# The third and fourth x tile are loaded behind the second half of the modulation weights, with row statistics of their own, and turned half a unit later

## The reference, cut to what matters

```python
def rms_norm(x, g):
    xf = x.astype(jnp.float32)
    y = xf * lax.rsqrt(jnp.mean(xf * xf, axis=-1, keepdims=True) + EPS)
    return (y * g.astype(jnp.float32)).astype(x.dtype)
...
    mod = c @ w_ada + b_ada                      # w_ada is (1024, 3072)
    shift, scale, gate = jnp.split(mod[:, None, :], 3, axis=-1)
    h = rms_norm(x, norm_g) * (1 + scale) + shift
    proj = h @ w_in
```

## Time and profile before

| | |
|---|---|
| median of 3 runs | 1639.85 us (1638.99 to 1643.24) |
| the profiled execution: its time | 1640.34 us |
| the profiled execution: its span | 1638.5 us |
| PE busy | 1602.0 us (98%) |
| DVE, ACT, POOL busy | 762.2, 595.2, 832.3 us |
| DMA over the span | 105 GB/s in the mean, 320 GB/s in the first fortieth |

### The profile page before, as it was taken

How to read it: one execution, slowest core, us unless ns; L and a number is a source line. 1 busy time by engine, 2 the same in 40 slices (tenths; PEclk the granted TensorE clock), 3 DMA queues, 4 the chain that set the end, 5 groups by cost and what they waited for, 6 DMA issues and landing times.

```text
span 1638.5 us, 31905 instructions
## 1 busy us (share of the span) xinstructions
PE 1602.0 (98%) x13096; PEld 1293.9 (79%) x13096; DVE 762.2 (47%) x1900; ACT 595.2 (36%) x1163; POOL 832.3 (51%) x1080
## 2 busy tenths in 40 slices
PE   5999999999999999999999999999999999999998
PEld 2787777877888777888878877788888977888886
DVE  3665444323458664522234764623345764533122
ACT  3334413334322552343432364243332364233230
POOL 2425333457674552446756363346677354346671
PEclk9999999999999999999999999999999999999999
DMA  9712212344554331233365231223455232122352
GB/s 320 225 53 78 65 41 66 90 129 116 167 155 110 97 91 41 66 103 112 95 181 130 54 102 53 63 69 116 128 172 162 65 89 67 54 73 84 97 162 70
DMA packets 303049, 172.65 MB, mean 105 GB/s; under 512 B 73774, under 2 KB 290183, under 8 KB 302888
## 3 DMA queue, kind: packets, MB, share of 16 engines
q1 hardware_dynamic: 302904, 170.61, 35.7%
HBM read 159.66 MB, written 11.96 MB: 105 GB/s over the span
## 4 chain that ended last, share of the span: by engine, by line
PE 93%; DVE 3%; SPq 2%; issue 1%; DMA 1%; ACT 1%; POOL 0%; DVEq 0%
PE ps_D L739 53%; PE ps_D L736 24%; PE ps_XB L907 2%; PE ps_XB L899 2%; PE ps_XD L792 2%; SPq L503 2%; PE ps_XA L893 1%; PE ps_XB L871 1%; PE ps_XB L922 1%; PE ps_XA L927 1%; PE ps_XB L921 1%; PE ps_XC L804 1%; PE ps_XA L871 1%; DMA th_t<-in_w_ada 1%; PE ps_XC L914 0%
## 5 line engine op out<-in xcount | busy, mean ns | idle before, releaser
L1642 POOL TENSOR_TENSOR w_lo_t<-w_raw,w_hi_t 128x256 fp32r<-128x256 f32 x928 | 680.9, 766 | 638.3 <-ACT w_hi_t L953 638.3
L739 PE MATMUL ps_D<-h_hi_t,w_hi_t 128*128 128x512 f32 x1024 | 415.1, 405 | 0.0
L739 PE MATMUL ps_D<-h_hi_t,w_lo_t 128*128 128x512 f32 x1024 | 400.5, 391 | 0.4 <-issue 0.4
L739 PE MATMUL ps_D<-h_lo_t,w_hi_t 128*128 128x512 f32 x1024 | 400.0, 391 | 0.0
L953 ACT ACTIVATE w_hi_t<-w_raw 128x1024 fp32r<-128x1024 f32 x232 | 240.2, 1052 | 74.8 <-PE ps_D L736 40.2
L739 PEld LDWEIGHTS ps_D<-h_hi_t,w_hi_t 128*128 128x128 f32 x1024 | 192.2, 188 | 51.1 <-issue 14.4
L739 PEld LDWEIGHTS ps_D<-h_hi_t,w_lo_t 128*128 128x128 f32 x1024 | 192.2, 188 | 43.2 <-issue 0.8
L739 PEld LDWEIGHTS ps_D<-h_lo_t,w_hi_t 128*128 128x128 f32 x1024 | 192.6, 188 | 36.0
L736 PE MATMUL ps_D<-w_hi_t,h_hi_t 128*128 128x384 f32 (+1 forms) x384 | 141.9, 370 | 1.6 <-POOL h_lo_t L1665 0.9
L736 PE MATMUL ps_D<-w_hi_t,h_lo_t 128*128 128x384 f32 (+1 forms) x384 | 136.6, 356 | 0.0
L736 PE MATMUL ps_D<-w_lo_t,h_hi_t 128*128 128x384 f32 (+1 forms) x384 | 136.4, 355 | 0.0
(11 more groups left out here) (393 smaller groups left out, 2435.6 us busy)
## 6 DMA issues: line engine op xcount, KB each, us to landing
w_raw<-in_w_in SPq DMA_DIRECT2D x72, 512.0 KB, 3.9
w_raw<-in_w_merge SPq DMA_DIRECT2D x64, 512.0 KB, 3.9
w_raw<-in_w_in SPq DMA_DIRECT2D x64, 256.0 KB, 3.8
w_raw<-in_w_out SPq DMA_DIRECT2D x32, 512.0 KB, 4.1
x_or_AT<-in_x_prompt SPq DMA_DIRECT2D x20, 512.0 KB, 5.1
w_raw<-in_w_proj_a SPq DMA_DIRECT2D x64, 128.0 KB, 2.9
w_raw<-in_w_proj_b SPq DMA_DIRECT2D x32, 256.0 KB, 3.2
xr<-in_x_prompt SPq DMA_DIRECT2D x16, 512.0 KB, 5.3
```

The lines of the kernel that those rows point to most:

```text
L739: ins = mm(bank[:, :], w[:, s0, k0 + k, :], a[:, k, :], start=go, stop=end)
L1642: ins = g_.tensor_tensor(w_lo[:, c, k:k + 2], w_raw[:, n % NRAW, k:k + 2], f32(w_hi[:, c, k:k + 2]), ALU.subtract)
```

## The change

Three things change. SP loads tile 2 and 3 of x behind the second half of the modulation weights. ACT makes their sums of squares and their scaling behind `h_high_half(1, 1)`, and DVE makes their row statistics in a second `row_scales` of two columns, which stands behind the decode rows' modulation. PE turns tile 2 behind the second half of unit 0 and tile 3 behind the first half of unit 1.

```diff
-put(0, 0, 0, "xturn", 2)
-put(0, 0, 1, "xturn", 3)
+put(0, 0, 1, "xturn", 2)
+put(0, 1, 0, "xturn", 3)
...
-            for t in range(NT):
-                load(x_p[t], x[P * t:P * t + P, :], ("x_in0", "x_in1", "p_x2", "p_x3")[t])
+            for t in (0, 1):
+                load(x_p[t], x[P * t:P * t + P, :], f"x_in{t}")
...
             for k in range(KT):
                 ada_load(k, 1)
+            for t in (2, 3):
+                load(x_p[t], x[P * t:P * t + P, :], f"p_x{t}")
             load(ones[:, :], A["c_ones"], "p_load2")
...
             def scale_x(it, t, src):
-                s.wait_ge("rstd", it + 2)
+                s.wait_ge("rstd", it + 3 if it >= 0 else 1 + t // 2)
...
             squares(x_p[1], 1, srow[:, :])
-            s.wait_ge("p_x2", 16)
-            squares(x_p[2], 2, srow[:, :])
-            s.wait_ge("p_x3", 16)
-            squares(x_p[3], 3, srow[:, :])
-            for t in range(NT):
+            for t in (0, 1):
                 scale_x(-1, t, x_p[t])
...
             h_high_half(0, 1), h_high_half(1, 1)
+            s.wait_ge("p_x2", 16)
+            squares(x_p[2], 2, srow[:, :])
+            s.wait_ge("p_x3", 16)
+            squares(x_p[3], 3, srow[:, :])
+            for t in (2, 3):
+                scale_x(-1, t, x_p[t])
...
-            def row_scales(it):
-                s.wait_ge("xst", 8 * (it + 2))
-                do(tt(xw3, xst[:, 0:8:2], xst[:, 1:8:2], ALU.add))
-                do(ts(xw3, xw3, 1.0 / D, EPS, ALU.mult, ALU.add))
-                rsqrt(rst, xw3, xw1, xw2)
-                do(ts(rst, rst, 1.0, None, ALU.mult), "rstd")
+            def row_scales(it, t0=0, n=NT):
+                s.wait_ge("xst", 8 * (it + 1) + 2 * (t0 + n))
+                r = slice(t0, t0 + n)
+                do(tt(xw3[:, r], xst[:, 2 * t0:2 * (t0 + n):2], xst[:, 2 * t0 + 1:2 * (t0 + n):2], ALU.add))
+                do(ts(xw3[:, r], xw3[:, r], 1.0 / D, EPS, ALU.mult, ALU.add))
+                rsqrt(rst[:, r], xw3[:, r], xw1[:, r], xw2[:, r])
+                do(ts(rst[:, r], rst[:, r], 1.0, None, ALU.mult), "rstd")
...
-            row_scales(-1)
+            row_scales(-1, 0, 2)
...
             do(tt(hS[:, :, 0:NS], hS[:, :, 0:NS], shift[:, :, 0:NS], ALU.add), "p_scale")
+            row_scales(-1, 2, 2)
             for t in (2, 3):
                 modulate_half(t, 0), modulate_half(t, 1)
```

## The result

The changed kernel takes 1648.33 us, the median of 5 runs (1648.22 to 1649.13); the kernel before, on the same chip, 1640.41 us, also the median of 5 (1638.99 to 1645.13). The ratio is 1.0044, 95% interval 1.0032 to 1.0056: slower by about 7.2 us (the medians themselves lie 7.9 apart). The prediction was 1648.0 (1644.5 to 1650.5), with 0.8 for slower.

The account below looks back on a forecast made before the run. Loads set the time up to 49.07 us, PE behind it. Loads -2.7, new wait, transposes and late `D0` +8.3, clock +2.5 make +8.1 us: 1648.0 us from the median, range 1644.5 to 1650.5.

Parts of the forecast that it names:

- Loads, -2.7 us: Prologue: two 512 KB tiles leave the queue ahead of the last weights, so everything waiting for these moves up 2.7 us.
- ACT's order, squares, row statistics, scaling: Behind ACT's last half of tile 1: squares 3.05, statistics 3.4, scaling 1.13 us; PE idles 5.4 us before tile 2's transposes.
- 3.4 us for the two-column statistics over 1.7: DVE's second `row_scales`: small instructions cost a fixed time each, so 3.4 us; 1.7 if width counted.
- `D0`: DVE empties unit 0's `D0` only after modulating tile 3, so unit 2 waits and starts at 63.9, 5.6 us late.
- The clock, +2.5 us: Behind 54.0 us: after PE's idle hole its clock halves for some 5 us, costing 2.5 us; bounds 0 to 5.3.
- The argument from the length of the hole: PE's new 5.4 us hole is over twice the 2.6 us one that halved the clock, so it should fall.
- The sum: Whole kernel: -2.7 loads, +8.3 for wait, transposes and late `D0`, +2.5 clock: +8.1 us, 1648.0 us.
- the cases within 0.3%: Time not measurably changed: part of the held clock, the swallowed delay and the wait that doesn't bind; chance 0.18.
- The held clock (0.13): Rival: PE's clock stays up through the new hole, leaving +5.6 us, 1645.5 us; chance 0.13.
- the swallowed delay: Rival: PE's waits behind 60 us give back 4.4 us, leaving +3.7, or +1.2 with the clock held; chance 0.05.
- the wait that doesn't bind: Rival: tile 2 is scaled by 48.6 us, so PE needn't wait; 1638.1 us; chance 0.04.
- the loads that land no earlier: Rival: weights land no earlier because the slowest DMA engine decides; +8.3 and 2.5 us stay, 1650.7 us; chance 0.04.

Follow-up runs that it names:

- the loads alone: Kernel before with only tile 2 and 3's loads moved behind the weights, into buffers nothing reads, those tiles set to constants: 1640.27 us, ratio 1.0001.
- Loads at the front: Changed kernel with the loads of tile 2 and 3 back where they stood before; late statistics and transposes kept: 1649.32 us, ratio 1.0057.
- one Newton step: Changed kernel with one Newton step in place of three for tile 2 and 3's row scales, 8 small DVE instructions fewer: 1645.58 us, ratio 1.0034.
- squares in the gap: Changed kernel with ACT's squares of tile 2 and 3 ahead of `h_high_half(0, 1)` and `(1, 1)`, in ACT's idle time: 1645.39 us, ratio 1.0032.
- `D0` left early: Changed kernel with ACT and DVE emptying unit 0's accumulator ahead of their work on tile 3: 1646.85 us, ratio 1.0036.
- 14 products that do nothing: Kernel before with 14 one-column products added: in PE's wait for the weights 1635.08 us, ratio 0.9970; or at 205 us 1636.94 us, ratio 0.9980.
- 28 short products in the changed kernel: Changed kernel plus 28 one-column products, 6 ahead of unit 0's second half, 22 ahead of tile 2's transposes: 1645.32 us, ratio 1.0036.
- the run with fillers of 512 columns: Changed kernel plus 28 unread 512-column products, 6 ahead of unit 0's second half, 22 ahead of tile 2's transposes: 1642.05 us, ratio 1.0006.

## Why the prediction was right

- **Loads, -2.7 us.** The last weights came at 37.99 in place of 40.33: 2.34. The second half of unit 0 started at 46.74, expected 46.4. Size right: in the six profiles of the changed kernel and its variants with the late loads the last pair came at 37.05 to 38.78, 37.5 in the mean, where 37.6 was said. A single profile can be off by 1 us here. But the run with the loads alone shows that the gain holds in full only because the change makes everything behind it late. Alone, half of it is given back at the next weight block, and the rest shows in no time.
- **ACT's order, squares, row statistics, scaling.** Expected the transposes of tile 2 at 54.0, released by ACT: 54.46, so released. The 0.46 are ACT's later start on the squares (46.65, said 46.4) and small handovers. Choosing 3.4 us for the two-column statistics over 1.7 was right: 49.78 to 53.17 is 3.39. Loads at the front and one Newton step each moved that start by what their term gives, squares in the gap moved the start of the statistics by it. Only the wait was shorter than said, 3.62 us and not over 5, because the low clock in unit 0, which the prediction did not foresee, held PE up meanwhile; that changes no sum. The 15 instructions were 17, which changes none either, since the term came from their whole time.
- **`D0`.** Expected 5.6 us from tile 3's transposes to unit 2: 5.66. The text took this for a term of its own; `D0` left early shows that little is won by curing it alone.
- **The clock, +2.5 us.** The mechanism was right, the size was not: PE worked 3.0 us at half clock, not 5, and this term measured 1.3 to 1.4 us. The argument from the length of the hole was weaker than it looked: the hole was 3.62 us and not 5.4, and the clock had been low in unit 0 and come back (0.95 in the mean of the hole) before it fell again. "HAM oscillation", in the page "TensorE: Matmul & The Clock Gate" of the Trainium skill, takes half of the slow time as the loss. From the 3.0 us here that makes an estimate of 1.5 us, and the trace, with 1.3 to 1.4, agrees.
- **The sum.** At unit 2 +7.40, where the steps gave +8.1. From unit 2 to the end of the span it is 1580.2 us before and 1580.4 after; another 0.3 us lie around the span. That the tail is the same owes something to chance: it has other stalls and another fall of the clock in the two kernels, which happen to weigh the same. That the median came within 0.3 us of the forecast is luck as well: the clock's term was 1.1 to 1.2 us too large, the transposes came 0.5 late, and the kernel before stood 0.6 us higher in its five runs than in the three that the forecast started from. Two slips in its arithmetic carry nothing: the low end of the forecast is 1645.95, not 1645.8, and the cases within 0.3% add up to 0.16.
- **Rivals.** The held clock (0.13) would have given 1646.9 by the measured price and is ruled out by the granted clock; the swallowed delay, the wait that doesn't bind and the loads that land no earlier by the rows above.

## What to carry to other kernels

A transfer moved behind others speeds up only what stood between its two places; what comes later in the queue waits for the same bytes. When an operand's load is moved, follow also the in-order engine that prepares it: here the later load cost nothing; ACT's and DVE's steps behind their other work, the transposes out of their hole and the clock behind the wait made the cost. And before a few us are laid to a change, look for waits that no engine ends: here they moved with the number of instructions, and 14 products that do nothing won 3 to 5 us.

## What the hardware showed unexpectedly

- **Stalls that hang on the number of instructions.** 128 products of 16 columns, that is 256 instructions with their weight loads, run in 1.3 us. In the eight kernels without extra products a packet of the instruction queue falls among them between 218 and 231 us, and PE stalls for 1.7 to 2.1 us; 14 products more, at 29 or at 205 us, remove the stall. Not every packet among such products brings one (1030.4 us in the kernel before). The Trainium skill, "Runtime: NRT & Kernel Launch", section "Instruction fetch mechanics", says that instructions come in blocks of 16 KiB, 256 each, and that the cost of a boundary is mostly hidden. This case's trace agrees with the block, by the page's part on DMA queues (packets, MB, share of 16 engines) of the changed kernel:

```profile
q8 instruction: 104, 1.70, 0.4%
```

  That is 16 KB a packet. If the fetch is what PE waits for, its cost is not hidden where the products are as short as here. That it is the fetch is read from packets and stalls together and is not shown: no run changed the fetch by itself, and why some packets bring no stall is open.
- **A fall of the clock behind such a stall.** In the changed kernel the clock falls behind the stall at 230 us; in the runs without that stall it doesn't:

```profile
226.00:230.00 4.00, 2.24 (x146) 1.00 0.07 17
230.00:234.00 4.00, 3.82 (x12) 0.69 0.42 122
234.00:238.00 4.00, 4.00 (x30) 0.89 0.00 0
```

  By halving, 0.31 and 0.11 of 4 us lost are 1.7 us. The kernel before has a stall of the same size at 222 us and no fall there, but one behind 492 us, where the changed kernel has none. Of the fourteen profiles two show two such falls, nine one, three none, and the runs of one kernel spread by 3 to 8 us (but 0.9 in the five of the changed kernel). A longer time often goes with a lower mean clock: with 28 short products in the changed kernel 1644.12 us at 0.995 and 1649.23 at 0.991. No run shows what decides whether the clock falls.
- **The clock fell under a busy PE.** With 14 products of one column in the wait for the weights PE had no idle time at all, and yet the granted clock went to 0.50, as with the empty wait. The 22 short products ahead of tile 2's transposes left no idle time either, and the clock was at 0.50 from 52 us on. In the run with fillers of 512 columns it came back to 1.00 (above).

```profile
28.80:33.80 5.00, 5.00 (x32) 0.63 1.05 388
33.80:36.00 2.20, 2.20 (x9) 0.50 1.05 387
```
